# Where the first V rows stand in a stream of expert gathers

## The reference

```python
q  = (h @ w_peer_q).reshape(n, 8, 2, 128)            # query projection, h = RMSNorm(x)
s1, s2 = q[:, :, 0] @ sub_keys[0].T, q[:, :, 1] @ sub_keys[1].T
# per token and head: the 16 best of s1, of s2, then of their 256 sums -> 16 expert numbers idx
gate = softmax(top_s)
a = einsum('nhkd,nd->nhk', peer_u[idx], h)           # 128 rows of 2048 for each token
w = gate * gelu(a)
y = x + einsum('nhk,nhkd->nd', w, peer_v[idx])       # 128 more
```

## Time and profile before

| | |
|---|---|
| median of 3 runs | 2729.97 us (2728.58 to 2734.72) |
| the profiled execution: its own time, its span | 2729.56 us, 2727.9 us |
| busy, share of the span: TensorE / VectorE / GpSimd / ScalarE | 89% / 55% / 33% / 13% |
| DMA: moved, mean rate | 919.23 MB, 337 GB/s |
| of these by GpSimd's gathers and page loads (queue q0) | 725.64 MB, 66.0% of 16 engines' span |

### The profile page before, as it was taken

The page is one execution under the profiler, slowest core; times in us unless marked ns, Lnnn a source line. Parts: engine busy times, 40 slices in busy tenths (PEclk is TensorE's granted clock), DMA queues, the critical chain, the costliest instruction groups (busy, mean ns, idle before and its releaser), DMA issues.

```text
span 2727.9 us, 27186 instructions
## 1 busy us (share of the span) xinstructions
PE 2441.1 (89%) x8853; PEld 1516.2 (56%) x8853; DVE 1493.1 (55%) x2370; ACT 351.2 (13%) x773; POOL 903.2 (33%) x889
## 2 busy tenths in 40 slices
PE   9999999899999999999996778777999597777777
PEld 7888886378666678888884323332443142232333
DVE  3599996741323222012478787875555556554543
ACT  2111000022222210001112110111111011111110
POOL 1122211100222200000156656564543565445542
PEclk9999999999999999999998999998889899999999
DMA  6699996755899955456598999999999999999998
GB/s 227 222 400 385 384 364 217 284 193 189 300 352 357 353 178 188 138 168 218 184 371 346 421 415 421 418 411 422 421 410 422 411 414 416 412 422 418 418 422 368
DMA packets 269443, 919.23 MB, mean 337 GB/s; under 512 B 16154, under 2 KB 122738, under 8 KB 200308
## 3 DMA queue, kind: packets, MB, share of 16 engines
q0 software_dynamic: 122448, 725.64, 66.0%
q1 hardware_dynamic: 133156, 164.93, 18.0%
q10 hardware_dynamic: 13728, 27.26, 2.7%
HBM read 909.08 MB, written 8.72 MB: 336 GB/s over the span
## 4 chain that ended last, share of the span: by engine, by line
PE 49%; DMA 25%; DVE 12%; POOL 7%; issue 6%; ACT 0%; DVEq 0%; POOLq 0%; ACTq 0%; SPq 0%
DMA sb_bregion<-in_peer_u_dram,sb_ring 14%; PE ps L699 14%; PE ps L807 13%; PE ps L819 6%; PE ps L689 4%; PE ps L794 3%; DMA sb_mkv<-in_peer_u_dram,sb_ring 3%; DVE sb_bregion L2024 3%; DMA sb_S<-in_peer_u_dram,sb_ring 3%; PE ps L907 2%; PE ps L1056 2%; DVE sb_mkv L2024 2%; POOL sb_bregion L558 2%; POOL sb_wring L558 1%; DMA sb_bregion<-in_peer_v_dram,sb_ring 1%
## 5 line engine op out<-in xcount | busy, mean ns | idle before, releaser
L1056 PE MATMUL ps<-sb_wring,sb_ring 128*128 128x512 f32 x992 | 457.4, 610 | 84.5 <-DMA sb_wring<-in_peer_v_dram,sb_ring 82.9
L2024 DVE CUSTOM_DVE_ANT_0 sb_bregion<-sb_bregion,sb_rows 128x2048 f32<-128x2048 f32 x128 | 293.4, 2293 | 216.3 <-DMA sb_bregion<-in_peer_u_dram,sb_ring 205.9
L699 PE MATMUL ps<-sb_hT,sb_wring 128*128 128x264 f32 x1792 | 408.6, 388 | 0.7 <-DMA sb_wring<-in_w_in_dram 0.6
L1056 PEld LDWEIGHTS ps<-sb_wring,sb_ring 128*128 128x128 f32 x992 | 186.4, 194 | 354.3 <-issue 263.2
L699 PEld LDWEIGHTS ps<-sb_hT,sb_wring 128*128 128x128 f32 x1792 | 338.5, 191 | 60.4 <-DMA sb_wring<-in_w_in_dram 2.1
L807 PE MATMUL ps<-sb_hT,sb_wring 128*128 128x264 f32 x1536 | 365.5, 389 | 1.6 <-DVEq L1416 1.6
L807 PEld LDWEIGHTS ps<-sb_hT,sb_wring 128*128 128x128 f32 x1536 | 287.1, 190 | 64.9 <-issue 16.4
L1056 PE MATMUL ps<-sb_oreg,sb_ring 128*128 128x512 f32 x496 | 241.1, 638 | 76.4 <-DMA sb_oreg<-in_peer_v_dram,sb_ring 54.9
L1056 PE MATMUL ps<-sb_hT,sb_ring 128*128 128x512 f32 x496 | 231.1, 612 | 55.3 <-DMA sb_hT<-in_peer_v_dram,sb_ring 47.3
L558 POOL DMA_INDIRECT sb_bregion<-in_peer_u_dram,sb_ring x132 | 184.4, 1397 | 222.4 <-DVEq L1416 174.9
L1056 PEld LDWEIGHTS ps<-sb_oreg,sb_ring 128*128 128x128 f32 x496 | 98.0, 204 | 218.0 <-issue 156.5
(11 more groups left out here) (367 smaller groups left out, 2488.7 us busy)
## 6 DMA issues: line engine op xcount, KB each, us to landing
sb_wring<-in_w_in_dram SPq DMA_DIRECT2D x26, 2048.0 KB, 11.1
sb_ring<-in_cache_k_dram POOLq DMA_DIRECT2D x64, 512.0 KB, 8.6
sb_mkv<-in_cache_k_dram POOLq DMA_DIRECT2D x64, 512.0 KB, 8.8
sb_wring<-in_w_in_dram SPq DMA_DIRECT2D x26, 1024.0 KB, 13.7
sb_wring<-in_w_in_dram ACTq DMA_DIRECT2D x26, 1024.0 KB, 14.3
sb_mkv<-in_cache_v_dram POOLq DMA_DIRECT2D x48, 512.0 KB, 7.1
sb_rows<-in_cache_v_dram POOLq DMA_DIRECT2D x47, 512.0 KB, 7.2
sb_wring<-in_w_mem_kv_dram SPq DMA_DIRECT2D x8, 2048.0 KB, 8.2
```

The source lines that it names most:

```text
L699: last = mm(ps[:, c, 0:NT], whalf[:, h, k % BC, c * P:(c + 1) * P], rhs[:, k, :], start=(k == 0), stop=(k == KC - 1))
L1056: last = mm(ps[:, 4 * t + q, :], diag[:, k % 4, :], e_slots[v % ER][:, q * 512:(q + 1) * 512], start=False, stop=q_stop, skip_group_check= ...
L2024: st(V.tensor_tensor_reduce(out=u_slots[n % UR], in0=u_slots[n % UR], in1=h2, scale=1.0, scalar=0.0, op0=ALU.mult, op1=ALU.add, accum_out= ...
```

## The change

The list `FIRST_V` names the U rows behind which each of the first eight V rows is gathered; the others follow evenly from the 37th U row. The weights of head 0 are made at the seventh dot of head 1 instead of the first of head 2; so that its Gelu is there, ScalarE takes the exponentials and the Gelu of head 0 between the pieces of the projection, behind pieces 5 and 11.

```diff
-        V_LEAD, V_LEFT = 34, 12
+        V_LEAD, V_LEFT = 37, 12
+        FIRST_V = [18, 20, 28, 29, 31, 32, 33, 34]
...
         def v_before(n):
 
-            return max(0, (n - V_LEAD + 1) * (V_SLOTS - V_LEFT) // (U_SLOTS - V_LEAD))
+            early = sum(first <= n for first in FIRST_V)
+            return max(early, ER + (n - V_LEAD + 1) * (V_SLOTS - V_LEFT - ER) // (U_SLOTS - V_LEAD))
...
+            stage_part(0)
+            stage_part(1)
+            keep_scores(0)
+            keep_scores(1)
+            for i in range(2, len(PQ_PARTS)):
+                stage_part(i)
+                keep_scores(i)
+                if i == 5:
+                    winners(0)
+                if i == 11:
+                    activations(0)
+
             v = 0
             for g in range(2 * PH):
 
-                diagonals(v, v_before(u_slot(g, TOPK - 1)))
-                v = v_before(u_slot(g, TOPK - 1))
-                activations(g)
+                last = v_before(u_slot(g, TOPK - 1)) if g != 1 else 4
+                diagonals(v, last)
+                v = last
+                if g:
+                    activations(g)
...
-                    if j == 0 and g == 2:
+                    if j == 6 and g == 1:
                         weigh(0)
```

More of the change, by code:

```diff
@@ L1340, in keep_scores @@
                 act.sem_inc(s["rows_taken"], 1)
[L1342 to L1348, removed]
             def activations(g):
@@ L1389, in diagonals @@
                         diagonal(v)
-            winners(0)
+            stage_part(0)
[9 more added lines that the diff above has]
+                    activations(0)
             v = 0
             for g in range(2 * PH):
-                diagonals(v, v_before(u_slot(g, TOPK - 1)))
-                v = v_before(u_slot(g, TOPK - 1))
-                activations(g)
+                last = v_before(u_slot(g, TOPK - 1)) if g != 1 else 4
[3 more added lines that the diff above has]
+                    activations(g)
                 if g + 1 < 2 * PH:
```

## The result

Median 2738.15 us of 15 runs (2733.83 to 2742.06) against 2729.52 us of the kernel before on the same chips (15 runs, 2726.04 to 2736.42); the ratio is 1.0027, 95% interval 1.0020 to 1.0034. The change makes the kernel slower by some 7.4 us (5.5 to 9.3). That lies in the range predicted, but the likeliest case was 2731.5 us, no difference that can be told.

The account below looks back on a forecast made before the run. The prediction took the stream of gathers, from about 1440 us to the end, as the bound; 2729.6 - 2.5 - 2.4 + 6.6 = 2731.3 us, stated as 2731.5 because the median shown was 0.4 higher, with a range of 2722 to 2740.

Parts of the forecast that it names:

- The bound: From about 1440 us to the end, the stream of gathers sets the time, at 2.49 us a row.
- The other edits: Head 0's exponential and Gelu between projection pieces on ScalarE, and its weights moved on VectorE: claimed to cost nothing.
- The tile turn: Behind U166, V144 waits for TensorE's row 136 with only four rows queued: 6.6 us lost, bounds 3.0 and 8.
- The early gain: Early V rows fill DMA room around the start of the gather stream: gains of 2.5 and 2.4 us.
- the hole (76 to 104 us): DMA idle before U24's data, near 1431.6 to 1440.8: V0 and V1 shrink it from 9.2 to 6.7, gaining 2.5 us.
- the slow stretch (104 to 132): Lower DMA rate at 1460 to 1480, regained by V rows between U rows: 2.4 us, bounds 0 and 3.5.
- Rival (c): GpSimd's issue paces U24 to U37 and nine V rows at 2.73 us a row: 2735.6 us; chance 0.14.
- Other waits of V on TensorE: Own rows and each head's weights: nine or more rows stand behind the event, so no further loss was counted.
- Rival (d): A second hole, of the first one's size, at another wait of V on TensorE: 2738 us; chance 0.08.
- The chances: For the whole change: 0.22 faster, 0.55 same, 0.23 slower.

Follow-up runs that it names:

- e4_scalar: Kernel before with only the ScalarE and VectorE edits (head 0's exponential, Gelu and weights moved), its gather order kept whole: 2729.45 us, ratio 1.0000.
- e1_turn: Changed kernel with the V rows' lead given back before the tile turn, so eight rows instead of four stand behind U166: 2731.51 us, ratio 1.0005.
- e5_lead: Kernel before with only a lead of V rows, so four rows stand behind U166; no early rows, no other edits: 2738.02 us, ratio 1.0022.
- e6_sample: Changed kernel with the sample rows added after the dot of U164 instead of U166, no gather moved: 2731.69 us, ratio 1.0000.
- e9_lead3: Changed kernel with one more V row of lead between U100 and U200, so two rows instead of four lie behind U166: 2742.93 us, ratio 1.0046.
- e3_both: Changed kernel with V rows also behind U35 and U36 and, after U160, the V count of the kernel before: 2725.24 us, ratio 0.9986.
- e2_route: Changed kernel with V rows also behind U35 and U36, so nine rows instead of seven lie behind U35: 2734.39 us, ratio 1.0012.

## Why the prediction went as it did

**The bound** held. From the first copy to the end of the trace, the other eleven traces differ from that of the kernel before by - 10.6 to + 11.4 us, and their accounts of the whole stream differ from its account by the same, within 1.0 us: what a version gains or loses is what its gather queue loses less or more. The other edits cost nothing that shows (e4_scalar).

**The tile turn** was right in place, mechanism and nearly in size: 6.6 us forecast, 7.1 more than before by the account of windows, 6.0 to 7.4 by e1_turn, e5_lead and e6_sample. A row behind U166 is worth some 2.6 us (e9_lead3), near the 2.49 used. Two small terms were off. The queue ran dry 8.2 us after the dot of U166 had begun, not 10.0: worked out at 2.49 us a row, the next row had been flowing for 1.8 us when the dot could start. And V144's data came after 17.1 us, not 16.6. The Trainium skill has the first: in DMA: Bandwidth & Descriptors, "Anatomy of one DMA", it puts the fixed part of such a transfer at about 2 us and says that most of it is the wait for the confirmation of the last write; the 1.8 worked out here agree. Together the two terms make the hole 17.1 - 8.2 = 8.9 us long, past the bound of 8; the account counts 7.1 because the kernel before lacks 1.6 us in the same 200 us.

**The early gain** was right in sum: 4.9 us forecast, 3.8 measured (e3_both, 1.4 to 6.0 by its interval). Over 52 to 132 us the traces without early rows lack 14.9, 18.0 and 15.4 us (before, e4_scalar, e5_lead), those with V0 and V1 behind U18 and U20 12.3, 10.7, 11.3, 11.5, 10.5 and 11.1 (after, e1_turn, e2_route, e3_both, e6_sample, e9_lead3); the means differ by 4.9. Of these the hole (76 to 104 us) has 2.6, where 2.5 was forecast, and the slow stretch (104 to 132) 1.5, where it was 2.4. In e4_scalar's trace U17's dot is already some 3 us late; without that trace the means differ by 3.9, and the hole has 2.3.

A single pair of traces does not show this split: from before to after the hole shrank by only 0.9 us. With the 4.1 of the start taken off, U24's data came 2.7 us later, near the forecast 2.5, but the queue ran dry only 3.6 us later, not the 5.0 of two rows.

**Rival (c)**, whose sign was gathers of 2.2 us and more past 1460, did not come. Of the 18 gathers from 1463.88 to 1504.36 in the changed kernel's trace, 16 take 0.94 to 0.96 us.

**The step that failed** is the count of places: "Other waits of V on TensorE ... have nine or more rows behind the event, by the same count." I counted only where V waits for TensorE, and took the even spacing from the 37th U row for a lead and nothing else. It also leaves U35 and U36 without a V row just where VectorE goes into a route, and there it is U that waits, for VectorE. Seven rows x 2.49 = 17.4 us, less the 1.8 found at the tile turn, are 15.6, against 19.5 us from the dot of U35 to U40's data: a hole of 3.9 us. The windows show 4.3 (the queue ran dry 15.2 us after that dot began), the account of windows 4.8, and two V rows close it (e2_route). The forecast's sum without it was + 1.7 us; with it, + 6.5, against 7.4 measured. Rival (d) had the time, 2738, and a second hole, but at a wait of V on TensorE and as long as the first (6.6). The range held the result only because its upper end was drawn from that rival; that (d) met the time is luck.

**The chances**: 0.23 for slower was too low. With a queue that sets the end, the rows behind every route should have been counted, not only those behind the waits for TensorE.

## What to carry to other kernels

When one queue sets the end, go through every event behind which the queue's issuer must wait (a route, a signal, a freed slot), count the transfers already issued behind it, and compare their time, less the lag of the landing signal (some 2 us here), with the time to the next issue's data. Moving transfers forward takes them from somewhere: look at the stretch that is left without them, and at the places further on where the lead brings the issuer sooner to a wait. Where a hole comes from too few transfers behind a signal, giving the signal sooner was as good here as moving the transfers (e6_sample, 7.4 us; e1_turn, 6.0).

## What the runs showed of the hardware that was not expected

The moment of the first gather's copy varied between 1343.45 and 1348.66 us over the twelve traces of kernels that are alike up to there. In the pair before and after the difference of 4.1 us comes about between 500 and 565 us, around the projection of the memory: there TensorE waited 1.53 us (before) and 4.10 us (after) for its weights' DMA, and the 96 matmuls behind that wait took 41.5 and 43.2 us. A single pair of spans can mislead by more than the effect studied here.
